# Another pace of dots and V rows in a hybrid decoder step with expert retrieval, and a first tile that searches all its heads itself

## The reference

```python
q_lat, c_kv, k_pe, rq, rk, rv, rg = jnp.split(rms_norm(x) @ w_in, offsets, -1)
mla_out = attend(q, k, v)                      # causal latent attention, 8 heads
ret_o, R_new = retention(rq, rk, rv, R0, chunk)
h = x + concat([mla_out, silu(rg) * head_group_norm(ret_o)]) @ w_o
xb = rms_norm(h)
q = (xb @ w_peer_q).reshape(n, 8, 2, 128)      # PEER: 8 heads, 16 experts each
v1, i1 = top_k(q[:, :, 0] @ sub_keys1.T, 16);  v2, i2 = top_k(q[:, :, 1] @ sub_keys2.T, 16)
vs, ic = top_k((v1[..., :, None] + v2[..., None, :]).reshape(n, 8, 256), 16)
experts = i1[ic // 16] * 128 + i2[ic % 16]     # of 16384 experts, rows of 1024
act = gelu(einsum('nd,nhkd->nhk', xb, peer_u[experts]))
y = h + einsum('nhk,nhkd->nd', softmax(vs) * act, peer_v[experts])
```

## Time and profile before

| | |
|---|---|
| runs | 3473.72, 3480.07, 3485.91 us; median 3480.07 |
| profiled execution | 3479.65 us, span 3477.9 us, mean granted clock of PE 0.803 |
| busy share | PE 71%, DVE 71%, POOL 61%, ACT 12% |
| DMA | 1321.87 MB, mean 380 GB/s; gathers 81.2%, SyncE's queue 15.7% of 16 engines' span |
| chain that ended last | PE 26%, DVE 23%, DMA 22%, POOL 17%, issue 9% |

### The profile page before, as it was taken

How to read it: one execution, slowest core, us unless ns; L and a number is a source line. 1 busy time by engine, 2 the same in 40 slices (tenths; PEclk the granted TensorE clock), 3 DMA queues, 4 the chain that set the end, 5 groups by cost and what they waited for, 6 DMA issues and landing times.

```text
span 3477.9 us, 37700 instructions
## 1 busy us (share of the span) xinstructions
PE 2486.0 (71%) x11828; PEld 1260.8 (36%) x11828; DVE 2468.6 (71%) x8388; ACT 432.7 (12%) x980; POOL 2135.6 (61%) x2118
## 2 busy tenths in 40 slices
PE   6768656888756687696666777697766776678567
PEld 5644124644432334362331234363331233324200
DVE  4587757768678886767578766777578766948652
ACT  1101000113101221111001110111101110000000
POOL 0136755566646665647756775647756775677876
PEclk8879677898877888898886778898887788775667
DMA  6479999999999999999999999999999999999999
GB/s 256 170 266 393 383 347 388 389 382 357 392 399 367 391 370 391 411 370 410 410 410 406 410 409 407 397 368 410 411 410 400 410 406 408 381 411 383 348 409 369
DMA packets 373386, 1321.87 MB, mean 380 GB/s; under 512 B 60962, under 2 KB 72418, under 8 KB 352962
## 3 DMA queue, kind: packets, MB, share of 16 engines
q0 software_dynamic: 304128, 1107.43, 81.2%
q1 hardware_dynamic: 69058, 212.03, 15.7%
HBM read 1311.41 MB, written 7.88 MB: 379 GB/s over the span
## 4 chain that ended last, share of the span: by engine, by line
PE 26%; DVE 23%; DMA 22%; POOL 17%; issue 9%; SPq 2%; ACT 1%; DVEq 0%; ACTq 0%
DMA u_ring<-up_rows,codes 10%; POOL v_ring L824 9%; POOL u_ring L811 8%; DMA v_ring<-down_rows,codesT 8%; PE ps L932 7%; DVE u_ring L1785 7%; PE ps L869 6%; DMA wbuf<-weights 4%; DVE arena L1751 3%; PE ps L922 3%; PE ps L1132 2%; PE ps L1185 2%; DVE idx L1751 1%; DVE top_c L1751 1%; DVE top_v L1751 1%
## 5 line engine op out<-in xcount | busy, mean ns | idle before, releaser
L1785 DVE CUSTOM_DVE_ANT_0 u_ring<-u_ring,xn 128x512 f32<-128x512 f32 x2112 | 1345.7, 686 | 510.7 <-DMA u_ring<-up_rows,codes 506.3
L811 POOL DMA_INDIRECT u_ring<-up_rows,codes x1056 | 1077.4, 1020 | 769.6 <-issue 291.8
L869 PE MATMUL ps<-v_ring,Z 128*32 128x512 f32 x4096 | 1082.6, 757 | 613.8 <-DMA v_ring<-down_rows,codesT 474.6
L824 POOL DMA_INDIRECT v_ring<-down_rows,codesT x1056 | 1057.0, 1001 | 559.0 <-issue 284.4
L869 PEld LDWEIGHTS ps<-v_ring,Z 128*32 128x32 f32 x4096 | 147.9, 121 | 1222.2 <-DMA v_ring<-down_rows,codesT 918.0
L1132 PEld LDWEIGHTS ps<-xT,wbuf 128*128 128x128 f32 x2176 | 312.0, 229 | 200.0 <-issue 119.1
L1132 PE MATMUL ps<-xT,wbuf 128*128 128x128 f32 (+1 forms) x2176 | 337.4, 318 | 57.1 <-DMA wbuf<-weights 57.1
L932 PE MATMUL ps<-wbuf,xT 128*128 128x256 f32 (+2 forms) x1184 | 285.4, 399 | 64.9 <-DMA wbuf<-weights 34.8
L932 PEld LDWEIGHTS ps<-wbuf,xT 128*128 128x128 f32 (+1 forms) x1184 | 226.4, 198 | 141.4 <-DMA wbuf<-weights 47.8
L1785 DVE DVE_READ_ACCUMULATOR2_ANT dots<- 128x1 f32 x2112 | 170.4, 81 | 0.0
L1751 DVE MAX8 vals<-arena 128x8 f32<-128x128 f32 (+1 forms) x288 | 68.8, 279 | 79.1 <-ACT arena L1565 78.4
(11 more groups left out here) (337 smaller groups left out, 2425.2 us busy)
## 6 DMA issues: line engine op xcount, KB each, us to landing
wbuf<-weights SPq DMA_DIRECT2D x142, 1024.0 KB, 8.2
u_ring<-up_rows,codes POOLq DMA_INDIRECT x1056, 12.3
v_ring<-down_rows,codesT POOLq DMA_INDIRECT x1056, 12.2
u_ring<-weights SPq DMA_DIRECT2D x8, 1024.0 KB, 13.5
v_ring<-weights SPq DMA_DIRECT2D x8, 1024.0 KB, 13.8
wbuf<-weights SPq DMA_DIRECT2D x9, 768.0 KB, 7.7
resid<-x_prompt SPq DMA_DIRECT2D x8, 512.0 KB
table<-decay_in SPq DMA_DIRECT2D x8, 512.0 KB
```

What stands on the lines that cost most here:

```text
L811: pool.indirect_dma_start(out=u_ring[:, i % U_RING, :], out_offset=None, in_=up_rows, in_offset=bass.IndirectOffsetOnAxis(ap=codes[:, t % ...
L824: pool.indirect_dma_start(out=v_ring[:, v % V_RING, :], out_offset=None, in_=down_rows, in_offset=bass.IndirectOffsetOnAxis(ap=codesT[:, t ...
L869: mm = pe.matmul(acc[q:q + 32, half, :], (Zs if t == TILES else Z)[:, at:at + GS], v_ring[:, v % V_RING, half * 512:(half + 1) * 512], sta ...
L1785: ins = dve.tensor_tensor_reduce(u, u, xn[:, t % 2, of], 1.0, 0.0, ALU.mult, ALU.add, into)
```

## The change

Only the pace lists and the place of two heads are changed; every gather, dot and product is still done.

- New lists. Slots of a stage, before and after: tile 1: project 23, 26; attention 12, 10; sample mixer 37, 21; out 11, 8. Tile 2: project 22, 33; qkv 12, 9; attention 12, 10; sample batch 37, 32. Tile 3: project 18, 25; attention 14, 11; sample batch 40, 36. Tiles 4 and 6: project 23, 34; qkv 15, 16; attention 40, 27; out 17, 18. Tiles 5 and 7: project 18, 26; qkv 18, 20; attention 43, 31; out 16, 18. The search keeps 33, the last stretch has 62 for 58.
- TURN_OVER = 5: slot 128 t lies one step later in the search, so each project stage begins at slot 128 (t-1) + 14, for + 18.
- Tile 0 has a list of its own for its search (FIRST_PEER): it begins at step 2, for step 4, and does 32 slots, for 18.
- Tile 0 searches heads 6 and 7 in its own search stage and asks and takes the gates there (`WHOLE`, and `t in (0, TILES - 1)`); tile 1's project stage has none of that.

```diff
--- before.py
+++ after.py
@@ -540,28 +540,35 @@
 
 
 
-        PROJECT = [3, 3, 4, 4, 3, 3]
-        QKV = [3, 2, 3, 3, 2, 2]
-        ATTEND = [4] * H + [5, 5]
+        PROJECT = [4, 4, 4, 5, 4, 4]
+        QKV = [2] * 6
+        ATTEND = [4] * H + [4, 4]
         OUT = [4, 4, 4, 2, 2, 2]
         FRONTS = {t: PROJECT + QKV + ATTEND + OUT for t in range(TILES)}
         for t in (4, 6):
-            FRONTS[t] = [3, 3, 4, 4, 4, 5] + QKV + [4] * H + [4, 4] + [4, 3, 4, 2, 2, 2]
+            FRONTS[t] = [4, 5, 5, 5, 8, 7] + [2, 3, 3, 2, 4, 2] + [3] * 7 + [2, 2, 2] + [5, 3, 3, 2, 3, 2]
         for t in (5, 7):
-            FRONTS[t] = [3, 3, 4, 4, 2, 2] + [3] * 6 + [4, 5, 4, 5, 4, 5, 4, 4] + [4, 4] + [4, 4, 2, 2, 2, 2]
-        FRONTS[1] = [3, 3, 4, 4, 4, 5] + [2] * 6 + [1] * H + [2, 2] + [4, 3, 4, 3, 4, 4, 4, 4, 3, 4] + [2, 2, 2, 2, 1, 2]
-        FRONTS[2] = [3, 3, 4, 4, 4, 4] + [2] * 6 + [1, 2, 1, 1, 2, 1, 1, 1, 1, 1] + [1] + [3, 2, 2] * BATCH + [2, 2, 2, 2] + [2, 2, 2, 2, 1, 2]
-        FRONTS[3] = [3, 3, 4, 4, 2, 2] + [2] * 6 + [1, 2, 1, 2, 1, 2, 1, 1, 2, 1] + [1] + [3, 3, 2] * BATCH + [2, 2, 2, 1] + [2, 2, 2, 2, 1, 2]
-        LAST = [9, 9, 5, 3, 3, 3] + [3, 3] * H + [2, 2] + [58]
+            FRONTS[t] = [2, 3, 7, 7, 3, 4] + [3, 4, 4, 3, 3, 3] + [3, 3, 3, 4, 3, 4, 3, 3, 3, 2] + [4, 4, 3, 2, 3, 2]
+        FRONTS[1] = [4, 4, 5, 5, 4, 4] + [2] * 6 + [1] * (H + 2) + [2, 2, 3, 2, 2, 2, 2, 2, 2, 2] + [2, 1, 2, 1, 1, 1]
+        FRONTS[2] = [4, 5, 5, 5, 7, 7] + [1, 2, 2, 1, 2, 1] + [1] * (H + 2) + [1] + [2, 2, 2] * BATCH + [2, 2, 2, 1] + [2, 2, 2, 2, 1, 2]
+        FRONTS[3] = [2, 3, 7, 7, 3, 3] + [2] * 6 + [1, 1, 2, 1, 1, 1, 1, 1, 1, 1] + [1] + [3, 2, 2] * BATCH + [2, 2, 2, 1] + [2, 2, 2, 2, 1, 2]
+        LAST = [9, 9, 5, 3, 3, 3] + [3, 3] * H + [2, 2] + [62]
         PEER = [[2, 2], [2, 2], [2, 1], [2, 2], [2, 2], [1, 2], [2, 2], [1, 2], [2, 2]]
-        TURN_OVER = 4
+        FIRST_PEER = [[0, 0], [0, 0], [0, 2], [3, 3], [3, 3], [3, 3], [2, 3], [2, 3], [1, 1]]
+        TURN_OVER = 5
 
         def sites():
 
             bounds = []
             for t in range(TILES + 1):
                 at = (t - 1) * SLOTS + sum(sum(two) for two in PEER[TURN_OVER:])
-                if t < TILES:
+                if t == 0:
+                    at, sizes, before, after = 0, [0] * len(FRONTS[0]), sum(FIRST_PEER, []), []
+                elif t == 1:
+                    at = sum(sum(two) for two in FIRST_PEER)
+                if t == 0:
+                    pass
+                elif t < TILES:
                     sizes = FRONTS[t]
                     before, after = sum(PEER[:TURN_OVER], []), sum(PEER[TURN_OVER:], [])
                 else:
@@ -1609,7 +1616,7 @@
                 for w in range(1, N_IN, 2):
                     if w == 1:
                         lat_squares(t, n)
-                    if w == 5 and t:
+                    if w == 5 and t >= 2:
                         gate_exps(t - 1, P)
                     if w >= 5:
                         slots()
@@ -1640,7 +1647,7 @@
                 if t in B_TILES:
                     sample_batch(B_TILES.index(t), slots)
                 out_and_peer(t, P, slots, P if t + 1 < TILES and t + 1 not in GUESTS else 0)
-                if t == TILES - 1:
+                if t in (0, TILES - 1):
                     gate_exps(t, P)
 
             def pages_turned(b):
@@ -2079,6 +2086,7 @@
                    over(ms8[0:n, 0:8], 2, [n, H, K]), ALU.mult)
 
             HEADS_HERE = 6
+            WHOLE = (0, TILES - 1, TILES)
 
             def out_and_peer(t, n, slots, following):
                 turned_copy(t, 1, n, None)
@@ -2090,7 +2098,7 @@
                 slots()
                 turned_copy(t, 2, n, None)
                 slots()
-                here = HEADS_HERE if t + 1 < TILES else H
+                here = H if t in WHOLE else HEADS_HERE
                 for s in range(H + 1):
                     if s == HEADS_HERE and following:
                         norm_in(t + 1, following)
@@ -2106,7 +2114,7 @@
 
             def project(t, n, slots):
                 def head_before(h):
-                    if t:
+                    if t >= 2:
                         peer(t - 1, h, P, lambda: None)
                 if t in GUESTS:
                     dve.wait_ge(tile_in, 48 * (t + 1))
```

## The result

| | before | after |
|---|---|---|
| median | 3473.05 us (3466.37 to 3485.91) | 3502.21 us (3499.39 to 3511.56) |
| profiled execution | 3479.65 us, span 3477.9 | 3499.39 us, span 3497.6 |
| mean granted clock of PE | 0.803 | 0.800 |
| busy share | PE 71%, DVE 71%, POOL 61%, ACT 12% | PE 71%, DVE 71%, POOL 61%, ACT 12% |
| DMA | 1321.87 MB at 380 GB/s | 1321.87 MB at 378 GB/s |

The ratio is 1.008, with an interval of 1.0061 to 1.0098. The forecast was 3469 us, with 3494 as the upper end. The two traces differ by 19.7 us where the sum said -10.8. What follows explains the 19.7.

A forecast was written before the change was run, and what follows sets the result against it. Idle DMA time, some 254 of 3477.9 us, was taken as all a new pace can win. The terms 9 - 8 - 2 - 17 - 3 + 10.2 = -10.8 took 3479.65 to 3469 us, range 3446 to 3494.

The forecast's parts named there:

- Tile 0 up to the queries of tile 1: Tile 0's search and tile 1's project: exposed heads and more slots put qkv at 338 us, +49.5 us.
- Tile 1's mixer: Tile 1's sample mixer: 16 slots fewer and no waits for U rows, 121.6 to 86 us, -35.6.
- the price of a slot that leaves qkv and attention: Qkv and attention of tiles 1 to 3: each slot removed saves DVE's 1.23 us.
- come out of full rings: Tile 2's project: 16 us of DMA for the added slots taken from rows already gathered, so PE's +5.3 decides.
- Tiles 2 and 3: All stages of both tiles with their new lists: -8 us for tile 2 and -2 for tile 3.
- Tiles 4 to 7: Project of tiles 4 and 6 loses its idle DMA time, -17 us in all; tiles 5 and 7 zero.
- the cover of 7 us: Attention of tiles 4 and 6: with fewer slots DMA still outlasts DVE and PE by 7 us, costing nothing.
- The handing: Boundary one head later: POOL's 62.6 us of waits for codesT go, -3 us, bounds 0 and -8.9.
- The tail: Last stretch: 4 slots more at 2.56 us of DMA each, +10.2 us.
- the first rival: Tile 1's mixer and out, and the sample batches, shrink too little to repay tile 0: 3500 us; chance 0.20.
- The rival by PE's clock: Host project stages: waits for weights lower PE's clock, at 0.76 10 us in each of three, 3499; chance 0.05.
- The rings hide it: Whole kernel: 22 us of rows in flight already even out the stages, so costs and gains cancel, 3480; chance 0.13.

The follow-up runs named there:

- e4_t23_c: Kernel before with the boundary one head later, last stretch 62 and the new lists of tiles 2 and 3: 3476.41 us, 1.0004.
- e1_tile0_b: Kernel before with tile 0's part alone (two heads, FIRST_PEER, tile 1's list), old boundary: 3498.02 us, 1.0059; in a slow session 3719.44, 1.0017.
- e7_two_heads: Kernel before with only heads 6 and 7 and the gates moved into tile 0's search stage, no list changed: 3512.74 us, 1.0114.
- e3_t4to7_c: Kernel before with the boundary one head later, last stretch 62 and new lists of tiles 4 to 7: 3469.41 us, 0.9983; slow session 3676.08, 0.9898.
- Y: The new lists of tiles 2 and 3 as one part, worked out from pairs of runs: some +4 us, give or take 6 to 8.
- e2_later: Kernel before with only the boundary one head later (TURN_OVER 5, last stretch 62), slow session: 3708.09 us, 0.9987.
- e6_whole_late: Whole change, but tile 0 does 18 slots from step 4 as before and tile 1's mixer 35 for 21: 3505.51 us, 1.0082 against before.

## Why the prediction was wrong

**Tile 0 up to the queries of tile 1: right.** The steps were 245 for xT, 250.5 for the first piece, 338 for qkv. The timelines of after, of DVE and then of PE:

```profile
243.82 0.69 DVE L1762 TENSOR_TENSOR xT<-ps,attn_wc 128x512 f32<-128x512 f32 x1 [0.25 <-DVEq L77]
```

```profile
248.01 3.63 PE L876 MATMUL ps<-v_ring,Z 128*32 128x512 f32 x12 [41.13 <-ACT Z L1373]
251.56 4.42 PE L939 MATMUL ps<-wbuf,xT 128*128 128x256 f32 x16
```

243.82, 251.56 and 341.67. PE stands 41.13 us ahead of its V rows, which is the exposed search. Of the missing 3.7 us, 1.1 are ahead of the first piece and 2.6 in the project stage, which took 90.1 us for 87.5. There PE waits 8.4 us for weight pieces, 2.5 before; the step had no such wait. The longest is this one:

```profile
297.79 5.19 PE L939 MATMUL ps<-wbuf,xT 128*128 128x256 f32 x16 [7.45 <-DMA wbuf<-weights]
```

**Tile 1's mixer: right.** From the same instruction on, 118.9 us fell to 84.1, -34.8 for -35.6 (bounds -19.6 and -41). Three rows of the view of waits of after, 398 to 489.5 us:

```profile
POOL v_ring L831 <- PE ps L876: 18.5, 6, 10.3
...
PE ps L1273 <- DVE vN L1762: 13.4, 1, 13.4
PEld ps L1313 <- DVE xT L1762: 13.1, 8, 3.3
```

The waits for U rows are gone from the list, as said; what is late next is the exchange of PE and DVE over vN and xT, and it left 14.5 us of DVE idle (84.1 - 69.6), where the step kept 12. Now DMA idles instead: 20.7 us (84.1 x (1 - 309 / 410)) for 9.6. The out stage fell 3.6 for 2.7, and PE still waits 8.34 us for its third weight piece, 11.47 before; SyncE's 32 stores of states still stand ahead of it, 17.00 us for 18.67 (PE's line, then SyncE's):

```profile
516.60 6.70 PE L939 MATMUL ps<-wbuf,xT 128*128 128x256 f32 x16 [8.34 <-DMA wbuf<-weights]
```

```profile
486.80 17.00 SPq L767 DMA_DIRECT2D R_sample<-kT  x32
```

**The step that failed in tiles 1 to 3: the price of a slot that leaves qkv and attention.** The out stage of tile 1 began at 489.5 us for 479, the turn for tile 2 came at 646.4 for 636. Only 3.7 us of that lie ahead of tile 1's queries. By stages, with PE's marks (queries, last product of the attention's values, turn of `mix`) in both traces:

| stage | before | after | measured | forecast |
|---|---|---|---|---|
| tile 1: qkv and attention | 60.3 | 63.7 | +3.4 | -2.4 |
| tile 1: mixer | 118.9 | 84.1 | -34.8 | -35.6 |
| tile 1: out and search | 159.9 | 156.9 | -3.0 | -2.7 |
| tile 2: project | 100.9 | 108.2 | +7.3 | +5.3 |
| tile 2: qkv and attention | 65.2 | 64.2 | -1.0 | -6.1 |
| tile 2: sample batch | 114.5 | 110.1 | -4.4 | -7 |
| tile 2: out and search | 147.9 | 146.1 | -1.8 | 0 |
| tile 3: project | 64.9 | 71.7 | +6.8 | +7 |
| tile 3: qkv and attention | 72.5 | 69.9 | -2.6 | -3.7 |
| tile 3: sample batch | 122.8 | 119.5 | -3.3 | -5 |
| tile 3: out and search | 141.5 | 138.7 | -2.8 | 0 |

Qkv and attention are 12 us over the forecast in the three tiles, the batches 4. The lines of qkv and attention, before and then after:

```profile
288.45:348.75 60.30, 44.19 (x255) 22.66 (x252) 53.88 (x173) 15.12 (x38) 46.58 (x46) 0.92 1.02 401
...
728.40:793.60 65.20, 50.10 (x283) 26.01 (x280) 56.85 (x178) 17.30 (x39) 50.23 (x50) 0.90 1.02 399
...
1120.90:1193.40 72.50, 55.02 (x313) 29.09 (x312) 64.90 (x198) 17.15 (x36) 53.18 (x54) 0.88 1.03 409
```

```profile
341.70:405.40 63.70, 43.72 (x249) 21.46 (x248) 53.87 (x173) 17.53 (x47) 47.59 (x47) 0.84 1.01 393
...
754.60:818.80 64.20, 51.11 (x262) 26.27 (x260) 53.76 (x167) 16.85 (x38) 46.24 (x46) 0.89 1.03 409
...
1146.70:1216.60 69.90, 56.76 (x302) 29.62 (x300) 60.75 (x186) 17.16 (x36) 53.03 (x53) 0.90 1.03 409
```

DMA is near full in all six, 393 to 409 GB/s, so these stages last as long as what POOL gathers in them, and that hardly fell. Counted from the timelines, POOL issued 45, 49 and 53 gathers before and 46, 45 and 53 after, while DVE and PE used 44, 46 and 52 rows before and 42, 38 and 47 after: 15 rows fewer are used and 3 fewer are gathered. The 12 between them refill the rings, an estimated 15 us of DMA (12 x 1.28). So what the fuller project stages take out of the rings, the stages behind them put back. The prediction let 16 us of tile 2's project "come out of full rings", priced the slots that leave qkv and attention at DVE's 1.23 us, and had no term for the refilling. The count fits the lengths; no run here varies the rings' size, so it is read from the traces and not tested by itself.

The batches did shrink, unlike what the text ahead of e4_t23_c assumes: they gave 4.4 and 3.3 us for 5 and 4 slots, 0.9 us each, where 1.23 to 1.5 was taken. DVE's idle time in them stays near 19 and 22 us; in tile 2's, PE's 24 waits for the tile `arena` from ACT add up to 16.5 us before and after. The alternation of the engines is the likely reason; no run isolates it.

**Tiles 2 and 3 in other runs.** From the turn for tile 2 to that for tile 4 before took 830 us, but e1_tile0_b and e7_two_heads, with the same lists there, 824 and 823, and e3_t4to7_c 821. With the new lists the fast traces have 825 to 833 (after 828). So one pair of traces can be 7 us off here, and the gain of 2 us in the table above is not one; the new lists give nothing where -10 was forecast. The times say the same: 1.0004 for e4_t23_c, Y = +4.

**Tiles 4 to 7: half, -7.3 for -17, and the lists give little of it.** The idle time of the hosts' project stages went, as said (411 and 404 GB/s, 111 us for 112). The attention is still at 410, so the cover of 7 us held. But e4_t23_c, which has the new boundary and the old lists in tiles 4 to 7, already takes 1553.4 us for them, against 1559.4 in before and 1551.9 with the new lists (e3_t4to7_c). Its lines for tile 4's project and search:

```profile
1453.40:1550.40 97.00, 89.05 (x440) 66.66 (x438) 59.90 (x218) 13.57 (x32) 48.50 (x49) 0.93 1.00 390
1742.30:1843.30 101.00, 72.04 (x424) 44.06 (x424) 82.75 (x326) 7.77 (x23) 54.56 (x56) 0.84 1.03 411
```

The boundary alone brought this project stage from 379 to 390 GB/s (tile 6's from 376 to 389), so there was less left for the lists to win. And what was not seen is who pays: the search, which had no idle DMA time in tile 4 before, now has some. The view of windows of before, for the search of tile 4, which answers to the line at 1760 above:

```profile
1746.70:1849.00 102.30, 73.59 (x420) 44.16 (x420) 82.12 (x324) 7.49 (x21) 54.14 (x55) 0.84 1.03 410
```

The searches of tiles 4 to 7 lose 3.0, 2.6, 3.4 and 4.5 us where they lost 0, 3.6, 0 and 2.7. This comes with the lists and not with the boundary: in tiles 4 and 6 e3_t4to7_c loses 3.0 and 3.6 us, e4_t23_c nothing (411 in both). In tile 4 the loss falls into the last 20 us of the search; before that both run at 406 to 416 GB/s. POOL stands equally long in both (4.0 us for dots, then 5.0 for PE's V rows), but only with the new lists does DMA run out of work meanwhile. Why it has less in hand there is not shown.

**The handing: -3 was not too much.** The 62.6 us of POOL's waits for codesT are gone to the last one, as forecast, and again in e3_t4to7_c and e4_t23_c. e2_later, 0.9987, can't settle 3 us: its interval is 7 us wide to either side, it ran in a slow session, and it holds the longer tail and four slots fewer in tile 0's search. The traces can: with the old lists tiles 4 to 7 are 4 to 6 us shorter with the new boundary (1553.4 us) than with the old (1557.8 in e1_tile0_b, 1558.8 in e7_two_heads, 1559.4 in before). That is inside the bounds of 0 and -8.9, but it is one trace against three, and whether the waits for codesT or the shifted places of the slots do it, these runs don't separate.

**The tail: right**, +9.9 for +10.2.

**The signs.** None of the three signs of being wrong came up: qkv of tile 1 at 341.7 us (limit 345), qkv and attention of tiles 4 to 7 at 402 GB/s or more (limit 400), host stages at a clock of 0.92 to 0.94 (limit 0.83). The out stage of tile 1 at 489.5 stayed below the 493 of the first rival. So the marks watched the parts that held, and none watched the refilling.

**The rivals.** The slower one named 3500, and the traces say 3499, but this is luck. It priced its case as mixer, attention and out of tile 1 falling by less than 30 us together, and as batches that don't shrink. They fell 35.0, nearly all of the 40.7 forecast, and the batches shrank by 7.7 us of 12. The rival by PE's clock is out: host stages at 0.92 to 0.94 for 0.93 to 0.96. The Trainium skill, "TensorE: Matmul & The Clock Gate", Part 1, has activity release the clock; full of gathers, tile 4's project left PE a little less busy, 96.72 of 111.10 us or 87% for 91%, and the clock fell from 0.95 to 0.92, the way the rule says but far from the 0.83 that would have cost time. "The rings hide it" named 3480 and was too low for the whole, but it comes nearest for the lists: moving slots inside a tile changed next to nothing.

**Where the 30 us went.** For tile 0's part with tile 1 the sum says +9, but with four slots fewer done; e1_tile0_b does them in its mixer, for 5 to 10 us (4 x 1.23 to 4 x 2.56), so +14 to +19 is to be compared with the +20.5 measured alone (1.0059). For the rest the sum says -8 - 2 - 17 - 3 + 10.2 = -20 and the same four slots less, -25 to -30; alone it measured -2 (0.9994). So the whole cost against before lies in tile 0's part, and it had been forecast nearly right; the miss lies in the lists, which were to pay for it and did not. By e7_two_heads the exposure itself is worth 37 to 40 us, and the early dots with a thinner mixer return some 19 of it (1.0114 to 1.0059).

What stays open is e6_whole_late against the whole change, 1.0082 and 1.0062: the intervals overlap, so the worth of the early dots within the whole change is only bounded; and that e7's loss would vanish with a longer V ring was not tried.

## What to carry to other kernels

What a stage takes out of full buffers is a loan: ask which stage puts it back, and count the transfers in the stages behind it (12 rows, some 15 us here), not only the work that left them. Work that ran under another engine's stage costs, once exposed, its own time and in addition all that the buffers cannot prefetch meanwhile (16.4 us of search became 37). Before two windows are compared, let both begin at the same instruction: what is looked for here is 4 us of 115, and a window that begins 4 us too early hides it. And where a kernel lives on the memory's rate, look at more than one session before a list is tuned by 0.3%.

## What the runs showed of the hardware

**Sessions differ in the rate of gathers, and the sign of a change with it.** The same bytes, the same kernel: 3473 to 3477 us in sessions where the last stretch runs at 406 to 410 GB/s, 3716 and 3743 us where it ran at 379 (e1_tile0) and 371 (the whole change), so that a slot costs an estimated 2.8 us of DMA (1.0486 MB / 0.375) instead of 2.56. The number of the chip does not decide it, since number 4 stands under a slow session and, later, under a fast one. Slices of the slow page go up and down, and one reaches 411. Page of e1_tile0 there:

```profile
GB/s 240 212 247 376 356 296 369 357 354 317 354 382 390 345 329 359 385 336 389 378 405 364 392 374 397 377 351 380 379 395 365 385 372 375 364 411 376 346 366 327
DMA packets 373386, 1321.87 MB, mean 357 GB/s; under 512 B 60962, under 2 KB 72418, under 8 KB 352962
```

There the change is worth 1.7% (0.9828), in the fast sessions it costs 0.6 to 0.8%. Tile 4 shows how, in two pairs of traces with the same boundary: its project stage, which PE sets, grows by 13 us with the new list in the slow session (102 to 115, e2_later to e3_t4to7) and by 14 in the fast one (97 to 111, e4_t23_c to e3_t4to7_c), but qkv and attention, which DMA sets, give back 28 us for the 12 slots that leave (159 to 131) and only 19 in the fast one (141 to 122). Windows of e2_later in the slow session, tile 4's project, then qkv and attention:

```profile
1552.00:1654.00 102.00, 89.38 (x437) 66.43 (x437) 59.58 (x216) 13.57 (x32) 48.99 (x50) 0.92 0.97 371
1654.00:1813.00 159.00, 100.11 (x472) 44.81 (x470) 99.58 (x303) 19.51 (x43) 106.25 (x110) 0.76 0.99 382
```

Why these sessions are slower no trace here tells. The Trainium skill, "HBM Reference", Specifications (TRN2), says that the two cores of a domain share its bandwidth, about 358 GB/s each when both stream, and more for a core alone. The span's mean of 357 would agree, slices at 405 and 411 speak against a fixed share; no run here shows what the neighbouring core did, so this stays open.
